# Expert products as four 32-column tiles with weight pieces of four experts, in a two-block transformer kernel

## The chip, the cores and the metric

The kernel runs on one core of a Trainium2 chip. The metric is the device time of one execution in microseconds.

## What is computed

Two transformer blocks on 256 tokens of width 1024 in float32. Block 1: attention with a forget gate beside a convolution, cross attention over 256 memory tokens, and a mixture of 32 experts. Block 2: a gated recurrence beside sparse attention, a wide MLP and a last gated product. The change touches the experts alone:

```python
gates = jnp.sum(jax.nn.one_hot(ids, N_EXPERTS) * w[..., None], axis=1).T   # each token: 2 of 32 experts
def expert_step(y, args):
    wg, wu, wd, ge = args                    # (1024, 512), (1024, 512), (512, 1024), (256,)
    out = (jax.nn.silu(t @ wg) * (t @ wu)) @ wd
    return y + ge[:, None] * out, None
y, _ = lax.scan(expert_step, jnp.zeros_like(t), (w_gate, w_up, w_down, gates))
```

Each expert has three matrices of 2.097 MB, 201 MB in all, each read once.

## The kernel before, in words

The program is raw: every engine has its own instruction list, and semaphores join them. Sums stand in eight PSUM banks (`ps`).

A token's place in its expert's list (`pos`) is worked out from the routing. Tokens of an expert are gathered by a product with a 0/1 matrix (`choose`), so that only they are multiplied: `CAP` = 64 places per expert. If the fullest expert (`busiest`) has more tokens, extra passes (`"more"`) run; with the given inputs its list is 26 long, so neither kernel runs them.

TensorE works on pairs of experts (`pair`, L759 to L805). For a pair n it does, in this order:
- `product` gate (L765): 8 row tiles of the 1024 inputs, for each a 128x64 block of gathered tokens (stationary) and 512 columns of the weights (moving). The two experts alternate and write the two halves of one bank (`ps[e * CAP:e * CAP + CAP, ...]`), that is, two column tiles of the array.
- `scatter` of the pair before (L778): four 128x512 matmuls that put expert outputs back to tokens, weighted by the gates; VectorE adds them to `x` (L1401). It has two banks, so the third and fourth wait for VectorE.
- `product` up, likewise; `gather` of the next pair (L749, 16 matmuls); four transposes of `hidden` (L792) and two of the weighted choice matrix (L798).
- `product` down: 4 row tiles, two banks of 512 columns.

ScalarE applies silu (L1889) and copies `hiddenT`, `spread` and the outputs out of PSUM (L1891 to L1896). A float32 matmul shows as two MATMUL and two LDWEIGHTS records in the trace.

**Weights.** SyncE loads one matrix of one expert per DMA (2.097 MB, `load_matrix`, L2111) into one of nine places of that size: three in the arena, six slots of the ring. Nine are loaded ahead, while block 1's last products still run. Each later one waits until the matrix that was in its place has been used; the semaphores for that count once per expert and product, and SyncE waits for both:

```python
sp.wait_ge(sem(f"{tag}_{used}_filled"), 2 * (PERIOD * group + u // 6 + 1))
```

The experts run in hardware loops of three pairs on each engine. After them SyncE waits for all products (`experts_done`), and then loads the weight units of block 2 (`load`, L2104, or by halves L2101): hq0 into slot 2, hq1 into slot 1, hf0 into slot 0, and the others as places come free. Block 2 starts with VectorE's norms (L1101 on) and TensorE's transposes (L516), then the product with hq0 (L555).

## Time and profile before

| | |
|---|---|
| median of 3 runs | 1447.36 us (1444.27 to 1447.55) |
| the profiled execution: its time | 1448.72 us |
| its span | 1446.9 us |
| TensorE busy | 1369.3 us (95%) |
| VectorE, ScalarE busy | 657.7, 414.7 us |
| granted TensorE clock, mean | 0.972 |
| HBM read | 330.4 MB, 229 GB/s over the span |
| chain that ended last | PE 85%, DVE 9%, ACT 2%, DMA 1%; L765 alone 23% |

In the profile PE is TensorE's matmul, PEld its weight load, DVE VectorE, ACT ScalarE, SP SyncE; SPq is SyncE's own queue. A granted clock of 1.00 is 2.4 GHz, 0.50 is 1.2 GHz.

### The profile page before, as it was taken

Reading aid. Unit: us, or ns where it says so; the run is one execution under the profiler, and the core shown is the slowest. Engines: PE = TensorE matmul, PEld = TensorE weight load, DVE = VectorE, ACT = ScalarE, POOL = GpSimd, SP = SyncE. Lnnn points to the kernel's source line nnn. Section 1 sums busy time; section 2 is a strip of 40 time slices with the busy share of each in tenths; the row PEclk is TensorE's granted clock in tenths of the full one; section 3 lists DMA queues with packets and bytes.
Section 4 is the critical chain, followed back from the end, with each engine's and each line's share of the span. In section 5 each row is a group of like instructions: output and inputs, shape, how many; then the busy total and the mean of one; then the engine's idle time right before and its main releaser. Section 6 shows DMA issues by size and latency. Waiting matters only on the chain.

```text
span 1446.9 us, 18297 instructions
## 1 busy us (share of the span) xinstructions
PE 1369.3 (95%) x7540; PEld 927.9 (64%) x7540; DVE 657.7 (45%) x1181; ACT 414.7 (29%) x626; POOL 14.1 (1%) x23
## 2 busy tenths in 40 slices
PE   6999999789999999999996999999999999999997
PEld 5977777454334443444333998887867746998873
DVE  3798532431122212121124358887656525655353
ACT  1343412101111111111111355634354302554322
POOL 2000000000000000000000000000000000000000
PEclk9997999889999999999998999999999999999999
DMA  8441464359999999999954153434433043455530
GB/s 332 176 159 75 168 248 166 143 222 401 420 427 425 425 419 426 426 423 425 421 232 176 54 193 119 158 132 146 186 135 117 1 167 117 175 182 194 206 145 29
DMA packets 26962, 332.45 MB, mean 230 GB/s; under 512 B 3184, under 2 KB 3472, under 8 KB 5008
## 3 DMA queue, kind: packets, MB, share of 16 engines
q1 hardware_dynamic: 25760, 328.49, 57.6%
q0 software_dynamic: 1136, 3.02, 0.6%
q8 instruction: 49, 0.80, 0.2%
q14 instruction: 17, 0.14, 0.0%
HBM read 330.44 MB, written 1.05 MB: 229 GB/s over the span
## 4 chain that ended last, share of the span: by engine, by line
PE 85%; DVE 9%; ACT 2%; issue 2%; DMA 1%; SPq 0%; DVEq 0%; ACTq 0%
PE ps L765 23%; PE ps L483 10%; PE ps L531 9%; PE ps L502 9%; PE ps L1016 6%; PE ps L555 6%; PE ps L749 5%; PE ps L778 4%; PE ps L446 2%; PE ps L845 2%; DVE arena L1193 1%; DVE parts L1149 1%; PE ps L607 1%; PE ps L578 1%; DMA ring<-in_units 1%
## 5 line engine op out<-in xcount | busy, mean ns | idle before, releaser
L765 PE MATMUL ps<-ring,arena 128*64 128x512 f32 x1008 | 260.8, 594 | 5.4 <-ACT arena L1891 5.4
L1149 DVE TENSOR_TENSOR parts<-ring,parts 128x2048 fp32r<-128x2048 f32 x76 | 173.5, 2290 | 156.7 <-ACT parts L1790 156.4
L1790 ACT CAST parts<-ring 128x2048 fp32r<-128x2048 f32 x76 | 144.4, 1904 | 178.1 <-PE ps L483 73.5
L502 PE MATMUL ps<-parts 128*128 128x512 f32 x768 | 181.6, 396 | 0.0
L765 PEld LDWEIGHTS ps<-ring,arena 128*64 128x64 f32 x1008 | 82.3, 137 | 144.4 <-issue 140.3
L483 PE MATMUL ps<-parts 128*128 128x256 f32 x1344 | 164.8, 285 | 3.1 <-DVE parts L1149 3.1
L483 PEld LDWEIGHTS ps<-parts 128*128 128x128 f32 x1344 | 163.4, 193 | 3.7 <-DVE parts L1149 2.1
L502 PEld LDWEIGHTS ps<-parts 128*128 128x128 f32 x768 | 145.7, 191 | 31.2 <-issue 1.1
L765 PE MATMUL ps<-arena 128*64 128x512 f32 x528 | 155.6, 594 | 3.3 <-ACT arena L1891 2.3
L1401 DVE TENSOR_TENSOR arena<-arena,ps 128x512 f32<-128x512 f32 x68 | 46.7, 687 | 236.8 <-PE ps L778 236.8
L531 PE MATMUL ps<-ring,arena 128*128 128x512 f32 x320 | 142.3, 602 | 4.4 <-issue 3.4
L531 PEld LDWEIGHTS ps<-ring,arena 128*128 128x128 f32 x320 | 60.9, 193 | 78.4 <-issue 77.2
L555 PE MATMUL ps<-arena,ring 128*128 128x128 f32 x768 | 93.9, 288 | 12.3 <-DMA ring<-in_units 6.9
L555 PEld LDWEIGHTS ps<-arena,ring 128*128 128x128 f32 x768 | 93.3, 204 | 14.2 <-issue 11.9
L765 PEld LDWEIGHTS ps<-arena 128*64 128x64 f32 x528 | 48.3, 137 | 79.6 <-issue 76.1
L1016 PE MATMUL ps<-parts 128*128 128x512 f32 x384 | 87.3, 389 | 0.0
L1016 PEld LDWEIGHTS ps<-parts 128*128 128x128 f32 x384 | 72.0, 188 | 14.9
L1891 ACT COPY arena<-ps 128x512 f32<-128x512 f32 x16 | 9.4, 585 | 230.6 <-PE ps L792 230.6
L749 PEld LDWEIGHTS ps<-arena 128*128 128x128 f32 x544 | 64.0, 197 | 15.0 <-issue 15.0
L749 PE MATMUL ps<-arena 128*128 128x128 f32 x544 | 67.2, 283 | 1.9 <-DVE arena L1380 1.9
L778 PE MATMUL ps<-arena 128*128 128x512 f32 x136 | 66.1, 618 | 1.3 <-ACT arena L1896 1.3
L1407 DVE TENSOR_TENSOR arena<-arena,ps 128x512 f32<-128x512 f32 x16 | 11.0, 687 | 101.9 <-PE ps L765 101.9
(313 smaller groups left out, 1231.3 us busy)
## 6 DMA issues: line engine op xcount, KB each, us to landing
ring<-in_units SPq DMA_DIRECT2D x43, 2048.0 KB, 7.7
ring<-in_w_down SPq DMA_DIRECT2D x22, 2048.0 KB, 12.9
ring<-in_w_up SPq DMA_DIRECT2D x21, 2048.0 KB, 12.0
ring<-in_w_gate SPq DMA_DIRECT2D x20, 2048.0 KB, 10.9
ring<-in_units SPq DMA_DIRECT2D x31, 1024.0 KB, 5.1
arena<-in_w_gate SPq DMA_DIRECT2D x12, 2048.0 KB, 11.5
arena<-in_w_up SPq DMA_DIRECT2D x11, 2048.0 KB, 11.4
arena<-in_w_down SPq DMA_DIRECT2D x10, 2048.0 KB, 12.1
```

What stands on the lines that cost most here:

```text
L446: mm = nc.tensor.matmul(bank, lhs[:, k, t * P:t * P + P], w[:, k, :], start=k == 0, stop=k == KT - 1)
L483: mm = nc.tensor.matmul(banks[f][:, half * T:half * T + T], w[:, k, at:at + P], v[:, 4 * h + k, :], start=h + half + k + n == 0, stop=h + ...
L502: mm = nc.tensor.matmul(banks[t], v[:, 4 * h + k, t * P:t * P + P], w[:, k, :], start=h + k + n == 0, stop=h == 1 and k == 3 and n == 2)
L531: mm = nc.tensor.matmul(bank, lhs[:, k, t * P:t * P + P], w[c][:, k, :], start=k == 0, stop=k == KT - 1)
L555: mm = nc.tensor.matmul(banks[u, c][:, to:to + P], w[u][:, k, at:at + P], rhs[:, k, t * P:t * P + P], start=k == 0, stop=k == KT - 1)
L749: mm = nc.tensor.matmul(ps[:, b, (k % 4) * P:(k % 4) * P + P], normed[:, t, k * P:k * P + P], choose[:, t, :], start=t == 0, stop=t == TT - 1)
L765: mm = nc.tensor.matmul(ps[e * CAP:e * CAP + CAP, bank, :], src[:, k, e * CAP:e * CAP + CAP], w[e][:, k, c * 512:c * 512 + 512], start=k = ...
L778: nc.tensor.matmul(ps[:, 5 + c, :], spread[:, t * P:t * P + P], expert_out[:, c * 512:c * 512 + 512], start=True, stop=True).then_inc(s("s ...
L1016: mm = nc.tensor.matmul(tiles[t], v[:, 4 * h + k, t * P:t * P + P], w[:, k, :], start=k4 + h + k + n == 0, stop=k4 == 3 and h == 1 and k = ...
L1149: step(V.tensor_tensor(rest_half(name, h), split_half(name, h), w_high[stage][h].bitcast(F32), ALU.subtract), f"{stage}_rest_ready", wait= ...
L1401: V.tensor_tensor(x[:, t, c * 512:c * 512 + 512], x[:, t, c * 512:c * 512 + 512], ps[:, 5 + c, :], ALU.add).then_inc(s("sum_drained"), 1)
L1790: step(S.copy(w_high[stage][h], split_half(name, h)), f"{stage}_high_ready", wait=False)
```

## The change

1. `CAP` goes from 64 to 32, and four experts (`SIDE` = 4, a quad; `QUADS` = 8) are worked on at once, as four 32-column tiles.
2. The weights are laid out anew on the host: a DMA brings a **piece** (2.097 MB as before), which holds two of the eight row tiles of gate or up for all four experts, or one of the four of down. 12 pieces to a quad, 96 in all, through the same nine places.
3. Each piece counts `piece_used` once per expert, and the next load into its place waits for that piece alone.
4. The scatter has four banks (`sum_banks`), and no wait inside. The choice matrices are built by one VectorE instruction instead of four.
5. The main expert stage is written out instead of looped (8 quads), on all engines.
6. SyncE issues the first three weight units of block 2 right behind the last piece, each after the last piece in its slot has been used, ahead of reading `busiest`.

```diff
-CAP = 64
+CAP = 32
+SIDE = P // CAP
-PAIRS = EXPERTS // 2
+QUADS = EXPERTS // SIDE
+PIECES = 12
...
+def quad_pieces(w, k):
+    n = w.shape[-1]
+    tiles = w.reshape(QUADS, SIDE, -1, k, P, n).transpose(0, 2, 4, 1, 3, 5)
+    return tiles.reshape(-1, P, SIDE * k * n)
...
-                    def product(group, r, first, tiles, name):
-                        src = hiddenT if first == 4 else picked
-                        for m in (6 * r + first, 6 * r + first + 1):
-                            landed, before = expert_landed(tag, m)
-                            pe.wait_ge(landed, before + 16 * (6 * PERIOD // N_PLACES * group + m // N_PLACES + 1))
-                        w = [expert_view(6 * r + first + e) for e in range(2)]
-                        n_k = src.shape[1]
-                        for c, bank in enumerate(tiles):
-                            for k in range(n_k):
-                                for e in range(2):
-                                    mm = nc.tensor.matmul(ps[e * CAP:e * CAP + CAP, bank, :], src[:, k, e * CAP:e * CAP + CAP],
-                                                          w[e][:, k, c * 512:c * 512 + 512], start=k == 0, stop=k == n_k - 1)
-                                    if c == len(tiles) - 1 and k == n_k - 1:
-                                        mm.then_inc(s(name), 1)
+                    def product(n, first, bank):
+                        for u in range(4):
+                            w = piece(n, first + u)
+                            for k in range(2):
+                                for e in range(SIDE):
+                                    mm = nc.tensor.matmul(ps[e * CAP:e * CAP + CAP, bank, :], picked[:, 2 * u + k, e * CAP:e * CAP + CAP],
+                                                          w[:, e, k, :], start=u + k == 0, stop=u == 3 and k == 1)
+                                    if k == 1:
+                                        mm.then_inc(s("piece_used"), 1)
...
+                    def down(n):
+                        pe.wait_ge(s("hiddenT_ready"), n + 1)
+                        for u in range(4):
+                            w = piece(n, 8 + u)
+                            for c in range(2):
+                                for e in range(SIDE):
+                                    mm = nc.tensor.matmul(ps[e * CAP:e * CAP + CAP, 3 + c, :], hiddenT[:, u, e * CAP:e * CAP + CAP],
+                                                          w[:, e, c, :], start=u == 0, stop=u == 3)
+                                    if c == 1:
+                                        mm.then_inc(s("piece_used"), 1)
...
-                                if t:
-                                    pe.wait_ge(s("sum_drained"), 4 * n + c + 1)
-                                nc.tensor.matmul(ps[:, 5 + c, :], spread[:, t * P:t * P + P],
+                                nc.tensor.matmul(ps[:, sum_banks[2 * t + c], :], spread[:, t * P:t * P + P],
...
+                    for n in range(QUADS):
                         pe.wait_ge(s("picked_drained"), 2 * n + 2)
+                        product(n, 0, 1)
+                        if n:
+                            scatter(n - 1)
+                        product(n, 4, 2)
+                        if n:
+                            pe.wait_ge(s("sum_drained"), 4 * n)
+                        if n + 1 < QUADS:
+                            gather(n + 1)
+                        turn_hidden(n)
+                        turn_spread(n)
+                        down(n)
+                    scatter(QUADS - 1)
...
-                load_pairs("moe", PAIRS)
+                n_places = places_of["moe"]
+                for m in range(n_places, PIECES * QUADS):
+                    sp.wait_ge(sem("moe_piece_used"), SIDE * (m - n_places + 1))
+                    load_piece("moe", m, m // PIECES, m % PIECES)
+                for n in range(n_early, n_early + 3):
+                    last_piece = max(m for m in range(PIECES * QUADS) if expert_places[m % n_places] == ("slot", units[n][2]))
+                    sp.wait_ge(sem("moe_piece_used"), SIDE * (last_piece + 1))
+                    load(n)
                 sp.wait_ge(sem("busiest_ready"), 1)
                 count = sp.value_load(busiest[0:1, 0:1], min_val=0, max_val=T)
-                experts_done("moe", PAIRS)
                 with sp.If(count > CAP):
```

TensorE, second group of experts, from its gate product over the scatter into the up product. Names in the rows: `moe_landed` and `weights_landed` are the semaphores of the places, and the loop of before shows each instruction once. Before:

```order
L759 REGISTER_ALU [waits moe_picked_drained]
L765 MATMUL ps<-ring,arena 64x512 [waits weights_landed1,weights_landed0]
L765 MATMUL ps<-ring,arena 64x512 x15
L778 MATMUL ps<-arena 128x512 [waits moe_out_ready,moe_spread_ready]
L778 MATMUL ps<-arena 128x512
L777 ISA
L778 MATMUL ps<-arena 128x512 [waits moe_sum_drained]
L777 REGISTER_ALU
L778 MATMUL ps<-arena 128x512 [waits moe_sum_drained]
L759 ISA [waits weights_landed2]
L765 MATMUL ps<-ring,arena 64x512 [waits moe_landed0]
```

Now, where `piece_used` is counted by the last matmuls of each piece:

```order
L777 MATMUL ps<-ring,arena 32x512 [waits weights_landed0]
L777 MATMUL ps<-ring,arena 32x512 x7
L814 MATMUL ps<-arena 128x512 [waits moe_out_ready,moe_spread_ready]
L814 MATMUL ps<-arena 128x512 x3
L777 MATMUL ps<-ring,arena 32x512 [waits weights_landed1]
L777 MATMUL ps<-ring,arena 32x512 x7
L777 MATMUL ps<-ring,arena 32x512 [waits weights_landed2]
L777 MATMUL ps<-ring,arena 32x512 x7
L777 MATMUL ps<-arena 32x512 [waits moe_landed0]
L777 MATMUL ps<-arena 32x512 x7
```

The product waits for one piece at a time instead of for two whole matrices, and the scatter's inner waits are gone.

SyncE, from the last of the nine loads ahead to the first that need a freed place. Before:

```order
L2111 DMA ring<-in_w_up 128x4096 [waits bank_filled3]
L2122 UNCONDITIONAL_BRANCH
L2122 ISA
L2111 ISA [waits moe_gate_filled]
L2111 DMA arena<-in_w_up 128x4096
L2111 ISA [waits moe_gate_filled]
L2111 DMA arena<-in_w_down 128x4096
L2111 DMA arena<-in_w_down 128x4096 [waits moe_up_filled]
```

Now:

```order
L2162 DMA ring<-in_w_up 128x4096 [waits bank_filled7]
L2162 DMA ring<-in_w_down 128x4096 [waits bank_filled3]
L2162 DMA arena<-in_w_down 128x4096 [waits moe_piece_used] x3
L2162 DMA ring<-in_w_gate 128x4096 [waits moe_piece_used] x4
L2162 DMA ring<-in_w_up 128x4096 [waits moe_piece_used] x2
L2162 DMA arena<-in_w_up 128x4096 [waits moe_piece_used] x2
```

The wait for a whole product of two experts has become a wait for one piece.

SyncE, from the last expert loads to the branch on `busiest`. Before (block 2's loads stand behind the branch):

```order
L2111 DMA ring<-in_w_up 128x4096 [waits moe_gate_filled]
L2111 DMA ring<-in_w_down 128x4096 [waits moe_gate_filled]
L2111 DMA ring<-in_w_down 128x4096 [waits moe_up_filled]
L2149 TENSOR_LOAD busiest [waits busiest_ready]
L2149 ISA x2
L2151 COMPARE_AND_BRANCH [waits moe_down_filled,moe_up_filled,moe_gate_filled]
```

Now:

```order
L2162 DMA arena<-in_w_down 128x4096 [waits moe_piece_used]
L2162 DMA ring<-in_w_down 128x4096 [waits moe_piece_used] x3
L2155 DMA ring<-in_units 128x4096 [waits moe_piece_used] x2
L2152 DMA ring<-in_units 128x2048 [waits moe_piece_used]
L2152 DMA ring<-in_units 128x2048
L2210 TENSOR_LOAD busiest [waits busiest_ready]
L2210 ISA x2
L2211 COMPARE_AND_BRANCH
```

Three units of block 2 (the third in two halves) stand ahead of the branch, and their only wait is for the pieces.

## Rows read from the trace of the kernel before

**Rows 1.** Page, 40 equal slices of the span (36.2 us each).
```profile
DMA  8441464359999999999954153434433043455530
GB/s 332 176 159 75 168 248 166 143 222 401 420 427 425 425 419 426 426 423 425 421 232 176 54 193 119 158 132 146 186 135 117 1 167 117 175 182 194 206 145 29
```

**Rows 2.** Windows: stretch, its us, busy us (instructions) per engine, granted clock, DMA share, GB/s.
```profile
275.00:280.00 5.00, 1.47 (x6) 0.90 (x5) 2.99 (x6) 0.20 (x1) 0.00 (x0) 0.77 0.70 223
280.00:285.00 5.00, 4.10 (x21) 3.73 (x19) 0.69 (x1) 3.02 (x8) 0.00 (x0) 0.50 1.03 439
295.00:300.00 5.00, 4.78 (x29) 4.58 (x28) 1.85 (x4) 1.28 (x1) 0.00 (x0) 0.69 0.00 0
305.00:310.00 5.00, 5.00 (x19) 1.84 (x16) 0.89 (x2) 0.60 (x1) 0.00 (x0) 1.00 0.25 52
330.00:335.00 5.00, 5.00 (x26) 1.78 (x24) 0.00 (x0) 2.36 (x3) 0.00 (x0) 1.00 0.71 229
335.00:740.00 405.00, 398.30 (x1942) 168.43 (x1938) 88.49 (x209) 51.03 (x81) 0.00 (x0) 1.00 1.01 424
740.00:745.00 5.00, 5.00 (x27) 1.59 (x24) 0.51 (x3) 0.00 (x0) 0.00 (x0) 1.00 0.63 265
745.00:775.00 30.00, 29.54 (x146) 12.38 (x144) 6.36 (x15) 3.81 (x6) 0.00 (x0) 1.00 0.00 1
```

**Rows 3.** Chain that ended last, one pair of experts: start us, us, what.
```profile
412.73 13.96 PE ps L765 x64
426.69 3.82 PE ps L778 x8
430.51 7.02 PE ps L765 x32
437.52 3.77 PE ps L749 x32
...
442.40 0.64 PE ps L765
```

**Rows 4.** Waits of TensorE (300 to 776 us) and SyncE: in total, times, longest.
```profile
PE ps L765 <- ACT arena L1891: 7.7, 16, 0.5
PE ps L765 <- DVE arena L1394: 1.0, 1, 1.0
...
SPq L2111 <- PE ps L765: 415.2, 44, 30.8
```

**Rows 5.** Timeline of SyncE and chain at the stage's start; loads of L2104 at 776.
```profile
300.76 1.04 PE ps L765 x3
...
308.04 0.35 SPq L2111 DMA_DIRECT2D arena<-in_w_up  x1
...
776.44 0.81 SPq L2104 DMA_DIRECT2D ring<-in_units  x2
...
DMA to landing us min/median/max: 8.0/10.6/13.1
```

**Rows 6.** Groups by line, 300 to 776 us: weight loads of the 64-column tiles.
```profile
L765 PEld LDWEIGHTS ps<-ring,arena 128*64 128x64 f32 x1008 | 82.3, 137 | 144.4 <-issue 140.3 <-ACT arena L1891 4.2
```

**Rows 7.** Page, DMA queue of the instruction fetches: packets, MB, share.
```profile
q8 instruction: 49, 0.80, 0.2%
```

**Rows 8.** Chain behind the last product of the experts.
```profile
773.97 2.20 PE ps L765 x10
...
776.82 0.46 ACT arena L1896
...
777.41 3.88 PE ps L778 x8
...
781.31 0.70 DVE arena L1401
...
783.22 1.22 DVE arena L1101
...
791.80 3.08 issue
```

More of the change, by code:

```diff
@@ L328, in two_blocks_kernel @@
                 before_experts = list(loads)
-                for m in range(6 * PAIRS):
-                    kind, at = expert_places[m % N_PLACES]
+                for m in range(PIECES * QUADS):
+                    kind, at = expert_places[m % places_of["moe"]]
                     if kind == "slot":
@@ L802, in experts @@
-                    with pe.Fori(0, n_pairs // PERIOD) as group:
-                        for r in range(PERIOD):
-                            pair(group, r)
-                    for r in range(n_pairs % PERIOD):
-                        pair(n_pairs // PERIOD, r)
-                    scatter(n_pairs)
-                    pe.wait_ge(s("sum_drained"), 4 * n_pairs + 4)
+                    return s, gather, product, turn_hidden, turn_spread, down, scatter
+                def experts():
+                    s, gather, product, turn_hidden, turn_spread, down, scatter = expert_steps("moe")
+                    gather(0)
+                    for n in range(QUADS):
+                        pe.wait_ge(s("picked_drained"), 2 * n + 2)
+                        product(n, 0, 1)
[10 more added lines that the diff above has]
+                    scatter(QUADS - 1)
+                    pe.wait_ge(s("sum_drained"), 4 * QUADS)
@@ new lines, in more_experts @@
+                def more_experts():
+                    s, gather, product, turn_hidden, turn_spread, down, scatter = expert_steps("more")
+                    with pe.Fori(0, MORE) as n:
+                        gather(n)
+                        pe.wait_ge(s("picked_drained"), 2 * n + 2)
+                        product(n, 0, 1)
+                        product(n, 4, 2)
+                        turn_hidden(n)
+                        turn_spread(n)
+                        down(n)
+                        scatter(n)
+                        pe.wait_ge(s("sum_drained"), 4 * n + 4)
@@ L816, in _ @@
                 with pe.If(count > CAP):
-                    experts("more", MORE)
+                    more_experts()
                 normed_half("mix2T", 0, 7)
@@ L1425, in experts @@
-                    drain_sums(n_pairs)
-                    dve.wait_ge(s("sum_drained"), 4 * n_pairs + 4)
-                experts("moe", 0, PAIRS)
+                    for n in range(QUADS):
+                        if n:
+                            drain_sums(n - 1)
+                        gate_hidden(n)
+                        if n + 1 < QUADS:
+                            drain_picked(n + 1)
+                            dve.wait_ge(s("spread_filled"), n + 1)
+                            build_gated(n + 1)
+                            dve.wait_ge(s("gated_choose_ready"), n + 2)
+                        if n + 2 < QUADS:
+                            build_choose(n + 2)
@@ L1429, in _, with more_experts @@
+                    drain_sums(QUADS - 1)
+                def more_experts():
+                    s, build_choose, build_gated, drain_picked, drain_sums, gate_hidden = expert_steps("more", QUADS)
+                    with dve.Fori(0, MORE) as n:
+                        build_choose(n)
+                        drain_picked(n)
+                        build_gated(n)
+                        gate_hidden(n)
+                        drain_sums(n)
+                experts()
                 count = dve.value_load(busiest[0:1, 0:1], min_val=0, max_val=T)
@@ L1430, in _ @@
                 with dve.If(count > CAP):
-                    experts("more", PAIRS, MORE)
+                    more_experts()
                 dve.wait_ge(sem("final_gain_landed"), 16)
@@ L1901, in _ @@
                 with act.If(count > CAP):
-                    experts("more", MORE)
+                    with act.Fori(0, MORE) as n:
+                        expert_quad("more", n)
                 for t in range(TT):
@@ new lines, in early_piece, with load_more_experts, load_next @@
+                def early_piece(m):
+                    load_piece("moe", m, m // PIECES, m % PIECES)
+                def load_more_experts():
+                    n_places = places_of["more"]
+                    def load_next(n, u):
+                        sp.wait_ge(sem("more_piece_used"), SIDE * (PIECES * n + u + 1))
+                        load_piece("more", u, n + (u + n_places) // PIECES, (u + n_places) % PIECES)
+                    sp.wait_ge(sem("moe_piece_used"), SIDE * PIECES * QUADS)
+                    for u in range(n_places):
+                        load_piece("more", u, 0, u)
+                    with sp.Fori(0, MORE - 1) as n:
+                        for u in range(PIECES):
+                            load_next(n, u)
+                    for u in range(PIECES - n_places):
+                        load_next(MORE - 1, u)
```

174 lines of the change are left out of this document (72 added, 102 removed).

## The prediction

> **What bounds the kernel now.** I read the page's slices first, then the windows of the expert stage, then the chain of waits inside it, then the waits of TensorE and SyncE. The slices show ten of the forty in which the DMA engines are full and move about 425 GB/s, with few others near that [rows 1]: this is the expert stage, a third of the span, and the change is in it. The windows put numbers on its two ends [rows 2]: from 335 to 740 us the DMA share is 1.01 at 424 GB/s, and TensorE is busy for 398.3 of 405 us. Both are full. Which of them sets the pace is told by the chain: it runs from one TensorE piece to the next, 13.96 + 3.82 + 7.02 + 3.77 us and some 1.1 us of transposes and handover, from 412.73 to 442.40: 29.67 us for a pair of experts [rows 3]. And TensorE's waits in the stage are 7.7 and 1.0 us in total, none for a DMA, while SyncE waits 415.2 us for TensorE's products to free a place [rows 4]. So TensorE is the bound, by a hair: six matrices of 2.097 MB in 29.67 us are 424 GB/s, just what the window shows.
>
> What TensorE costs is seen at the ends. SyncE's first load that needs a freed place goes out at 308.04, though the first product starts at 300.76, since a place comes free only after the whole gate product of two experts [rows 5]. The DMA engines rest between about 295 and 309 us (share 0.00, then 0.25), and again from 743 to 776 us (0.63, then 0.00), where all weights have landed and TensorE still works through a backlog [rows 2]. Block 2's loads go out at 776.44.
>
> **The sum.** It is made inside the profiled execution (span 1446.9, its own time 1448.7; the median of the runs shown is 1447.4, 1.3 lower, so the same difference is taken from the median).
>
> *TensorE's work per byte.* Two experts as 64-column tiles run side by side: 64 records of 128x512 take 13.96 us, 0.436 us for two. The change gives four tiles. If all four run side by side, a product of four experts takes the 7.0 us that two take now, and a group of four takes the 29.7 us of a pair, for twice the bytes. A weight piece (16 records) then takes 1.75 us. The trace has no 32-column tile, so the cost is bounded: below by 1.75 us; with never more than two at once 3.5 us; with no overlap 7.0 us; and if the 16 weight loads went singly, 16 x 137 ns = 2.2 us [rows 6]. A piece of 2.097 MB at 424 GB/s needs 4.95 us. In every case but the third the group (12 pieces plus about 8.8 us for gather, scatter, transposes and handover) stays under 12 x 4.95 = 59.4 us, and TensorE, the bound now, ends with slack: the DMA rate becomes the bound. I take 1.75, as the pair row shows full overlap of two.
> The Trainium skill (TensorE: Matmul & The Clock Gate, Part 3) gives 2.38x for three column tiles, short of 3x, which would make a piece 2.2 us instead of 1.75 and the sum 0.5 us longer; no run here shows it.
>
> *The start.* The choice matrix is now one VectorE instruction for four; worth a few tenths at most, taken as nothing. The first product starts at 300.8, its first piece is used at 302.5, and the first bound load goes out there instead of at 308.04: 5.5 us earlier. Pieces are used every 1.75 us against 4.95 us of transfer, so the dip at 330 to 335 us (229 GB/s) goes too.
>
> *The transfers.* 96 pieces less 9 preloaded are 87: 182.4 MB, at 424 GB/s 430.3 us [rows 2]. Two 2 MB loads into idle engines took at least 8.0 us each to land [rows 5], 3.1 more than 4.95. The last piece lands at 302.5 + 3.1 + 430.3 = 735.9. The same rule gives 308.0 + 3.1 + 430.3 + 2.3 (the dip) = 743.7 for the kernel before, where the DMA engines fell silent at 743.1. The loops written out bring more instruction fetches, about ten of 16 KB more (now 49 in the whole program, 0.80 MB [rows 7]): 0.2 MB, 0.4 us. Together 736.3.
>
> *The tail.* Behind the last product stand the two copies, the scatter, the last sum and VectorE's branch: in the trace 776.2 to 783.22, 7.0 us, of it 3.88 for the scatter [rows 8]. The last piece's product costs 1.75 us ahead of that, at full clock. But TensorE now works 1.75 of each 4.95 us. The granted clock was 0.77 in 275 to 280 us, where TensorE was busy 1.47 of 5, stayed at 0.50 in 280 to 285 with 4.10 of 5, and rose in 295 to 300 with 4.78 [rows 2]. So I take the lower level, 1.2 GHz, for the tail: the product 3.5 and the scatter 6.9 us (8 records at twice the 0.43 of full clock). At that level a group needs some 60 us of TensorE, about the 59.4 of its transfers; TensorE would then be busy without a break, and the clock would rise again, so the stage itself is not lengthened, and nine places cover the swings. Block 2's first instruction (L1101) starts at 736.3 + 3.5 + 1.2 + 6.9 + 0.7 + 1.2 = 749.8 instead of 783.22: 33.4 us saved, 38.6 at full clock.
> The Trainium skill (TensorE: Matmul & The Clock Gate, HAM oscillation) says that bursts of matmuls with a DMA wait between each find the clock low again every time; by it the low tail holds, and the trace's rows agree as far as they go.
>
> *Block 2's start.* Its first three weight units are queued behind piece 95 and land some 5, 10 and 15 us after it, by 751; TensorE wants the first about 8.6 us after L1101, at 758. Nothing waits for them, and nothing waited for them before either: their early issue is worth nothing by itself. But the chain has 3.08 us of "issue" at 791.80 that no engine releases, while the DMA engines are full with these units [rows 8]; I read it as an instruction fetch behind them, and with the queue empty by then I take half of it back: 1.5 us (bounds 0 and 3.1). The rest of block 2 is the same work, merely earlier.
>
> Sum: 33.4 + 1.5 = 35 us. 1448.7 - 35 = 1413.7 for a profiled run, 1447.4 - 35 = **1412.4** for the median.
>
> **The rivals.**
> *Warm tail (0.15).* The clock stays at 2.4 GHz: 5.2 us less, 1407. For it: a burst comes every 5 us; against it: the rows above.
> *The transfers run slower when never relieved (0.20).* Now leading DMA engines may catch their breath in the small slack; with the queue always eight deep the slowest engine sets the pace, and each of the ten added fetches delays one engine by about 1 us (0.2% of 16 engines' span over 49 packets). If all fall to the same engine this is 10 us; if the rate is 415 instead of 424 GB/s, 9 us. Time about 1423, at the worst 1430. For it: a DMA share of 1.01 leaves nothing in reserve; against it: 405 us at a flat 424.
> *Code starves TensorE (0.03).* If stalls like the 3.08 us one come with each of some 15 fetches of the stage and are not hidden, they cost 46 us against 35 won: about 1458, slower. Against it: a group has 29 us of slack for two such stalls, so they hide.
> *32-column tiles don't overlap (0.03), the slower end.* A piece costs 7.0 us, a group 12 x 7.0 + 8.8 = 92.8 us, the stage 742 instead of 475: about 1715. It decides from 4.2 us per piece (59.4 less 8.8, over 12). Overlap of two alone is not enough to get there: 50.8 us a group, and only 1.75 us more in the tail.
> *The change doesn't apply.* An expert with more than 32 tokens would call the extra passes, 56 groups of 59 us. From the given inputs the fullest expert has 26 tokens, so this is left out.
>
> **How the numbers follow.** The forecast case has 0.59 and its own range is 1406 to 1419 (rate 421 to 428 GB/s, the stall, the tiles at two). With the warm tail below and the slower transfers above, the range that should hold 8 in 10 is 1401 to 1427. A difference of 0.3% (4.3 us) is about what a measurement of this kernel can tell from none. Faster by more than that: 0.59 + 0.15 + 0.20 = 0.94; within: 0.01, a stretch between the cases in which stalls eat the gain; slower: the last two priced, 0.05.
>
> **What would show it.** Right: TensorE's largest waits in the stage are for DMA; SyncE's first load after a freed place near 302.5; DMA share 1.0 without a dip from there to 751, so that the idle stretch before block 2's loads is gone; TensorE busy near 50 to 70% with the clock under 1 in the stage; four L777 products inside 0.44 us at full clock; L1101 near 750. Wrong: landings further apart than 4.95 us, TensorE still without DMA waits, a piece over 4.2 us, or a gain that appears outside the stage.

## The result and the profile after

The changed kernel takes **1406.28 us** (median of 4 runs, 1399.48 to 1411.02) against 1447.4: a ratio of 0.9721, with a 95% interval of 0.9701 to 0.9741. The forecast was 1412.4, its range 1401 to 1427. The profiled execution is the fastest of the four: 1399.48 us, span 1397.2. Busy are TensorE 1180.7 us (1369.3 before), VectorE 593.5 (657.7), ScalarE 375.3 (414.7); the mean granted clock is 0.934 (0.972).

The page's slices (34.9 us each), to hold against [rows 1], with the granted clock; and the queue of the instruction fetches, against [rows 7]:

```profile
PEclk9997999979878989888788999999999999999999
DMA  9432283279999999999993443443441034445440
GB/s 342 183 127 115 98 324 127 78 304 428 427 428 428 427 428 428 427 428 427 428 427 148 146 170 121 154 143 127 181 181 61 32 142 159 187 187 190 182 151 30
...
q8 instruction: 58, 0.95, 0.3%
```

Twelve slices at 427 or 428 GB/s instead of eleven of 401 to 427; under them the clock wavers. The windows, against [rows 2] (stretch, its us, busy us of PE, PEld, DVE, ACT, POOL with their instructions, granted clock, DMA share, GB/s):

```profile
300.00:305.00 5.00, 5.00 (x48) 1.58 (x52) 0.70 (x2) 0.00 (x0) 0.00 (x0) 1.00 0.37 115
305.00:310.00 5.00, 5.00 (x52) 1.54 (x48) 0.00 (x0) 1.88 (x2) 0.00 (x0) 1.00 1.03 433
...
330.00:335.00 5.00, 1.92 (x16) 0.42 (x16) 0.00 (x0) 0.00 (x0) 0.00 (x0) 1.00 1.01 433
335.00:720.00 385.00, 247.78 (x1542) 74.79 (x1546) 36.85 (x58) 16.54 (x33) 0.00 (x0) 0.84 1.01 428
...
745.00:750.00 5.00, 1.47 (x7) 1.50 (x8) 4.43 (x9) 0.29 (x2) 0.00 (x0) 0.51 0.23 93
```

The full run of the DMA engines starts in 300 to 305 and has no dip at 330; it holds 428 GB/s. TensorE, busy for 398.3 of 405 us before, is busy for 247.8 of 385 us. In 745 to 750 the DMA engines fall silent with block 2's first units loaded. Before, they stood idle from 743 to 776 us.

The waits of TensorE in the stage (in total, times, longest), against [rows 4], and SyncE's longest one:

```profile
PE ps L777 <- DMA ring<-in_w_gate: 41.4, 19, 3.1
...
PE ps L803 <- DMA ring<-in_w_down: 30.3, 14, 3.0
...
PE ps L777 <- DMA arena<-in_w_up: 22.0, 8, 3.0
...
SPq L2162 <- PE ps L777: 262.7, 59, 24.8
```

TensorE waits for weights; before it never did. At the stage's start the chain (start us, us, what) and SyncE's timeline, against [rows 3] and [rows 5]:

```profile
299.99 13.94 PE ps L777 x128
313.93 3.77 PE ps L757 x32
...
302.06 3.76 SPq L2162 DMA_DIRECT2D arena<-in_w_down  x3
```

128 records of 32-column tiles take 13.94 us, what 64 records of 64-column tiles took before: **four tiles run side by side in full**. The first bound load goes out at 302.06 instead of 308.04. And the tail, against [rows 8]:

```profile
693.08 40.55 DMA ring<-in_w_down
...
733.67 2.05 PE ps L803 x16
...
736.96 3.69 PE ps L814 x8
...
742.57 1.22 DVE arena L1144
...
751.15 1.30 issue
752.45 2.69 PE ps L565 x11
```

The chain now runs through a DMA: the last piece, issued at 693.08, is there at 733.63. Its product, the copies, the scatter and the last sum follow, and block 2 starts at 742.57 instead of 783.22: 40.65 us earlier. Its first product starts at 752.45 instead of 794.88, 42.4 us earlier. The span is shorter by 49.7 us, so 7 us of this one trace come from behind, where nothing was changed. A gain outside the stage was one of the prediction's signs of being wrong; here it is a matter of this execution, as the repeats show.

### The profile page after: what moved, and what is told of

The parts are those of the page before. It is cut to its first block, busy times and chain, and to the rows that moved or that the text cites. A ratio compares the mean times of both kernels' runs of the same rounds, so it can differ in the third digit from the quotient of the medians.

```text
span 1397.2 us, 16587 instructions
## 1 busy us (share of the span) xinstructions
PE 1180.7 (85%) x7132; PEld 813.6 (58%) x7132; DVE 593.5 (42%) x992; ACT 375.3 (27%) x571; POOL 14.1 (1%) x23
## 4 chain that ended last, share of the span: by engine, by line
PE 59%; DMA 27%; DVE 10%; issue 2%; ACT 2%; SPq 0%; DVEq 0%; ACTq 0%
PE ps L493 10%; PE ps L541 9%; DMA ring<-in_w_up 9%; DMA ring<-in_w_gate 9%; PE ps L512 9%; PE ps L1059 6%; DMA ring<-in_w_down 6%; PE ps L565 6%; PE ps L777 3%; DMA arena<-in_w_up 3%; PE ps L456 2%; PE ps L888 2%; DVE arena L1236 1%; DVE parts L1192 1%; PE ps L617 1%
## 5 line engine op out<-in xcount | busy, mean ns | idle before, releaser
L777 PE MATMUL ps<-ring,arena 128*32 128x512 f32 x688 | 108.3, 763 | 65.7 <-DMA ring<-in_w_gate 41.4
L1437 DVE TENSOR_TENSOR arena<-arena,ps 128x512 f32<-128x512 f32 x32 | 22.0, 689 | 262.0 <-PE ps L814 261.9
L777 PEld LDWEIGHTS ps<-ring,arena 128*32 128x32 f32 x688 | 21.8, 125 | 148.8 <-issue 56.7
L565 PE MATMUL ps<-arena,ring 128*128 128x128 f32 x768 | 91.0, 282 | 11.2 <-DMA ring<-in_units 7.4
L565 PEld LDWEIGHTS ps<-arena,ring 128*128 128x128 f32 x768 | 90.2, 199 | 13.3 <-issue 11.0
L777 PE MATMUL ps<-arena 128*32 128x512 f32 x336 | 48.3, 704 | 37.8 <-DMA arena<-in_w_up 22.0
L803 PE MATMUL ps<-ring,arena 128*32 128x512 f32 x320 | 47.5, 721 | 32.6 <-DMA ring<-in_w_down 30.3
L1444 DVE TENSOR_TENSOR arena<-arena,ps 128x512 f32<-128x512 f32 x8 | 5.5, 688 | 120.2 <-PE ps L777 120.2
L777 PEld LDWEIGHTS ps<-arena 128*32 128x32 f32 x336 | 10.0, 117 | 75.1 <-DMA arena<-in_w_up 31.4
L1940 ACT COPY arena<-ps 128x512 f32<-128x512 f32 x8 | 4.7, 585 | 167.6 <-PE ps L786 167.6
L1236 DVE SCALAR_TENSOR_TENSOR arena<-arena,cols 128x256 f32<-128x256 f32 x120 | 48.6, 479 | 0.0
L803 PEld LDWEIGHTS ps<-ring,arena 128*32 128x32 f32 x320 | 9.3, 119 | 64.5 <-DMA ring<-in_w_down 46.0
```

What stands on the lines that cost most here:

```text
L565: mm = nc.tensor.matmul(banks[u, c][:, to:to + P], w[u][:, k, at:at + P], rhs[:, k, t * P:t * P + P], start=k == 0, stop=k == KT - 1)
L777: mm = nc.tensor.matmul(ps[e * CAP:e * CAP + CAP, bank, :], picked[:, 2 * u + k, e * CAP:e * CAP + CAP], w[:, e, k, :], start=u + k == 0, ...
L803: mm = nc.tensor.matmul(ps[e * CAP:e * CAP + CAP, 3 + c, :], hiddenT[:, u, e * CAP:e * CAP + CAP], w[:, e, c, :], start=u == 0, stop=u == 3)
L1236: ins = V.scalar_tensor_tensor(out=conv[:, cb, :], in0=z[:, cb, w:w + T], scalar=tap(w, cb), in1=conv[:, cb, :], op0=ALU.mult, op1=ALU.add)
```

## Experiments

Each edit is against the changed kernel unless another is named. There were twelve runs in three groups, each group on one chip beside the kernel before. The first group (a repeat of the changed kernel, the coarse wait, the late and the early units) and the third (a second repeat, the doubled and the tripled matmuls, the fillers at both ends) hold the changed kernel itself. The second (expert by expert, half loads, fillers at the start, fillers at the tail) does not, so its runs are compared with the changed kernel only by way of their ratios to the kernel before.

### The changed kernel, again

> The changed kernel again, unaltered, for a second trace of it and as the yardstick of the runs beside it. Theory (the transfers pace the expert stage): TensorE waits for DMA in the stage, the last piece lands near 733, and single times spread over some 10 us, because the granted clock falls and rises many times in the stage and its level in the tail, at 735 us, and in block 2 differs from run to run. The scatter then takes 3.7 us in one run and up to 6.9 in another. Rival (the first profile is typical, the spread is noise of the DMA rate): the tail is alike in both traces and the landing of the last piece moves by several us instead.

> The changed kernel once more, on the same chip as the three beside it, as their yardstick and for a third trace: median 1405 to 1410, single times spread over 10 us, with the level of the clock at 735 us and in block 2 going along with the time.

Medians 1408.57 (1402.78 to 1408.88, 5 runs, ratio to before 0.9709 to 0.9745) and 1407.73 us (1398.75 to 1409.68, 6 runs, 0.9697 to 0.9745). The second repeat's trace is of a run of 1408.11 us. Its chain at the tail:

```profile
732.01 3.01 PE ps L803 x16
...
736.26 5.36 PE ps L814 x8
...
743.54 1.22 DVE arena L1144
```

The last piece is there at 731.97, 1.7 us before that of the first trace (its loads began at 300.29, 1.8 us earlier); but product and scatter take 3.01 + 5.36 us against 2.05 + 3.69. In the first repeat the tail is as in the first trace, in the second it is slower. So the theory holds: the landing is steady, the clock is what changes. Block 2, from L1144 to the end of the span, took 1397.2 - 742.57 = 654.6 us in the first trace, 1400.5 - 741.24 = 659.3 in the first repeat and 1405.8 - 743.54 = 662.3 in the second. One window over the whole of block 2, first trace and then second repeat:

```profile
742.00:1397.00 655.00, 623.19 (x3730) 508.90 (x3730) 378.75 (x565) 265.74 (x380) 5.89 (x9) 0.98 0.37 138
```

```profile
742.00:1406.00 664.00, 631.02 (x3730) 514.91 (x3730) 379.04 (x566) 265.81 (x380) 5.91 (x9) 0.97 0.37 135
```

The same 3730 matmul records keep TensorE busy 7.8 us longer, at a mean clock of 0.97 instead of 0.98, while VectorE and ScalarE are busy for the same time in both. So what differs is how long the clock was low. The 662.3 us is the usual length: six of the variants below have 662.0 to 663.0. The kernel before had 1446.9 - 783.22 = 663.7. **So 7 to 8 us of the first trace's gain belong to that one run; the medians' 39 to 41 us are those of the stage.**

### When a place is given back

```diff
-                    sp.wait_ge(sem("moe_piece_used"), SIDE * (m - n_places + 1))
+                    sp.wait_ge(sem("moe_piece_used"), SIDE * (4 * ((m - n_places) // 4) + 4))
```

> A load waits again until the whole product (four pieces) that used its place is done, not the one piece; the rest is the changed kernel. Theory (the DMA rate bounds the stage and what counts is when its unbroken run begins): the first such load goes out 5.2 us later, near 307 instead of 302, the DMA engines stay full afterwards, and the whole is 5 us slower. Rival 1 (nine places absorb it): within 1 us. Rival 2 (the queue runs dry in each group, with only five to eight places in flight): slower by 2 us or more per group, 15 to 40 us in all.

1413.65 us (1413.18 to 1414.87), 5.1 slower than the repeat beside it (1408.57); ratio to before 0.9753 to 0.9785, against the repeat's 0.9709 to 0.9745, so clear of it. SyncE's first bound load in it, and its last piece's product:

```profile
304.93 1.28 SPq L2162 DMA_DIRECT2D arena<-in_w_down  x3
...
736.58 3.76 PE ps L803 x16
...
749.35 1.22 DVE arena L1144
```

4.05 us later than in the first repeat (300.88) and the last landing at 736.54 instead of 732.3, 4.2 us later. What the start lost came out at the end, no more and no less, so both rivals fall: nine places don't absorb it, and the queue doesn't run dry. (The 5.2 us expected are there too: the load goes out 7.21 us after the first product's start at 297.72, in the repeat 2.06 us after it; but that product happened to start 1.1 us earlier in this trace.)

### Block 2's units, late in the new kernel and early in the old

```diff
-                for n in range(n_early, n_early + 3):
-                    last_piece = max(m for m in range(PIECES * QUADS) if expert_places[m % n_places] == ("slot", units[n][2]))
-                    sp.wait_ge(sem("moe_piece_used"), SIDE * (last_piece + 1))
-                    load(n)
...
+                sp.wait_ge(sem("moe_piece_used"), SIDE * PIECES * QUADS)
+                for n in range(n_early, len(units)):
```

> The three weight units of block 2 are issued behind the branch on the fullest expert again, as in the kernel before, after all pieces are used; the rest is the changed kernel. Theory (early units are worth little, since TensorE wants the first of them 16 us after the last piece's product): 0 to 2.5 us slower than the changed kernel, all of it in the wait ahead of the first product of block 2 (1.3 us of issue there now, 3.1 before the change). Rival (the early units are a part of the gain, by filling the DMA engines' idle time): slower by 5 to 10 us, with TensorE waiting for ring<-in_units at the start of block 2.

1407.37 us (1405.47 to 1409.26), ratio to before 0.9706 to 0.9738: no difference from the repeat (1408.57). The units went out at 736.40 instead of 706.36, and TensorE's pause ahead of block 2's first product was 1.31 us, as with early units (1.30). **This part of the change is worth nothing that these runs can tell.**

The same part alone in the kernel before (the units behind `load_pairs`, each when the matrix in its slot is used):

```diff
                 load_pairs("moe", PAIRS)
+                for n, used in ((n_early, "down"), (n_early + 1, "down"), (n_early + 2, "up")):
+                    sp.wait_ge(sem(f"moe_{used}_filled"), 2 * (PAIRS - 1))
+                    load(n)
```

> The kernel before with nothing changed but that its three first units of block 2 are issued right behind the last expert matrix, as the change does. Theory: the gain of the change is not here; what goes is the 3.1 us of issue ahead of the first product of block 2, which I read as an instruction fetch that stands behind 6 MB of unit loads: 1.5 to 3 us faster than the kernel before. Rival (the units themselves are waited for): more than 5 us faster. Second rival (that stall has nothing to do with the DMA queue): no difference, and the 3.1 us still there.

1446.17 us against 1447.26, ratio 0.9996 (0.9987 to 1.0004): the second rival's "no difference" for the time, the theory for the pause. The DMA engines were idle by then (window 775 to 790), and the pause fell from 3.08 to 1.63 us:

```profile
775.00:790.00 15.00, 5.82 (x16) 2.80 (x16) 10.82 (x20) 2.92 (x8) 0.00 (x0) 0.80 0.01 3
...
789.39 1.63 issue
791.02 8.76 PE ps L555 x64
```

The late units above don't speak against a fetch behind the loads. In the kernel before the DMA engines were full for the first part of the pause, which began at 791.80; with late units in the changed kernel they had just run empty when it began, at 753.30 (first row before, second row late units):

```profile
792.00:793.00 1.00, 0.00 (x0) 0.00 (x0) 0.97 (x3) 0.00 (x0) 0.00 (x0) 0.50 0.99 410
...
753.00:754.00 1.00, 0.00 (x0) 0.00 (x0) 0.97 (x2) 0.29 (x2) 0.00 (x0) 0.50 0.14 57
```

So the pause was long in the one trace in which it met full DMA engines, and 1.30 to 1.63 us where it didn't. That it is an instruction fetch is not shown. With early units in the kernel before it is 1.45 us shorter; the interval allows the whole a gain of 1.9 us at most.

### How much TensorE may cost

Expert by expert inside a piece:

```diff
-                            for k in range(2):
-                                for e in range(SIDE):
+                            for e in range(SIDE):
+                                for k in range(2):
...
-                            for c in range(2):
-                                for e in range(SIDE):
+                            for e in range(SIDE):
+                                for c in range(2):
```

> Inside a piece the eight matmuls are issued expert by expert instead of row tile by row tile, so that two in a row go to the same 32-column tile. Same work, same loads. Theory (the gain rests on four tiles running side by side; TensorE becomes the bound from 4.2 us per piece): matmuls to one tile don't overlap, neighbours of two tiles do, a piece costs five steps of 0.86 = 4.3 us; a group costs about 60 us, no more than its transfers by 1 us, and the time grows by 0 to 15 us, with the clock at full level nearly throughout. Rival (a second matmul to the same tile stops all tiles): 7.0 us per piece, 93 us per group, 260 us slower. Rival 2 (order doesn't matter, the array takes what is ready): 1.75 us per piece, no change.

1407.76 us (1406.89 to 1410.43), ratio to before 0.9715 to 0.975, against 0.9697 to 0.9745 of the repeats: no change. My theory of this run fell and its second rival stands. The chain of its first two products:

```profile
300.07 14.01 PE ps L777 x128
```

128 records in 14.01 us. Two matmuls in a row to one tile don't hold up those of the next tile, as far as this time tells. As a test of the turning point the run is void.

Weights loaded by half (the matmuls of both row tiles, in the down product those of both banks, take the same half of the weights):

```diff
-                    src = by_piece[u // 4][:, bass.ds(4 * (quad % QUADS) + u % 4, 1), :]
-                    sp.dma_start(expert_flat(tag, m).unsqueeze(1), src)
+                    src = by_piece[u // 4][:, bass.ds(4 * (quad % QUADS) + u % 4, 1), 0:SLOT // 2]
+                    sp.dma_start(expert_flat(tag, m)[:, 0:SLOT // 2].unsqueeze(1), src)
...
-                                                          w[:, e, k, :], start=u + k == 0, stop=u == 3 and k == 1)
+                                                          w[:, e, :], start=u + k == 0, stop=u == 3 and k == 1)
```

> Each expert piece is loaded by half (1 MB), and the matmuls take their weights from that half, so the expert outputs are not those of the reference; the count of matmuls, waits and loads is the same. Theory (DMA bytes pace the stage): the stage shrinks from 433 to about 240 us, where TensorE (29.7 us per group at full clock) and the transfers (12 x 2.45 = 29.4 us) are level again, and the whole takes about 1215 us. Rival (a fixed cost per load or the instruction stream paces it): the stage shrinks by less than 100 us.

1202.45 us (one run, 13 less than expected), some 205 us less than the changed kernel; the last product ends at 530.3 instead of 735.7. The chain is TensorE alone again, one group of four from 407.77 to 437.23, 29.46 us where I had worked out 29.7:

```profile
407.77 7.07 PE ps L803 x64
414.85 6.87 PE ps L777 x64
421.71 3.63 PE ps L814 x8
425.34 7.01 PE ps L777 x64
432.35 3.77 PE ps L757 x32
...
437.23 2.77 PE ps L803 x23
```

So bytes pace the changed kernel's stage, and no fixed cost per load or instruction does.

Each expert matmul issued twice, and three times:

```diff
-                                for e in range(SIDE):
+                                for r, e in [(r, e) for r in range(3) for e in range(SIDE)]:
...
-                                                          w[:, e, k, :], start=u + k == 0, stop=u == 3 and k == 1)
-                                    if k == 1:
+                                                          w[:, e, k, :], start=u + k + r == 0, stop=u == 3 and k == 1 and r == 2)
+                                    if k == 1 and r == 2:
```

> Every matmul of the expert products is issued twice (the sums are doubled, so the expert outputs are not the reference's); loads and waits are as in the changed kernel. A piece then costs TensorE 3.5 us, a group 12 x 3.5 + 8.8 = 50.8 us against 59 us of transfers. Theory (the transfers pace the stage, TensorE has 29 us per group to spare): the last piece lands as before near 733, the clock stays at 2.4 GHz to the end of the stage, and the time is within 3 us of the changed kernel's 1406 to 1409. Rival (TensorE's work is still on the path in part): 20 us slower or more.

> Every matmul of the expert products is issued three times (sums tripled, outputs not the reference's). A piece costs 5.2 us, above the 4.2 us at which I put the turn: a group 12 x 5.2 + 8.8 = 71.6 us. Theory: TensorE is the bound again, its waits for DMA are gone, the stage takes 8 x 71.6 = 573 instead of 436 us, the whole about 1542 us. Rival (the turn lies higher, some of the repeats overlap as the matmuls of one tile did beside those of others): under 1450 us.

Twice: 1412.56 us (1404.52 to 1413.55, ratio 0.9722 to 0.9779), 4.8 more than the repeat beside it (1407.73), with intervals that overlap; the theory had said within 3 us of 1406 to 1409. The last piece landed at 736.94, not 733. Its first bound load went out at 302.48, 2.2 us later than the repeat's, and from there to the last landing it took 2.8 us more, which I put down, without a test, to places given back more slowly at the start. The window shows the clock:

```profile
335.00:720.00 385.00, 345.29 (x2936) 117.65 (x2932) 36.13 (x57) 16.86 (x33) 0.00 (x0) 1.00 1.01 427
```

TensorE is busy for 345 of 385 us, the clock is 1.00, and the transfers still go at 427 GB/s. The added 97 us of TensorE's busy time between 335 and 720 cost some 5 in all.

This run also tells which part of TensorE's saving is needed. With every matmul doubled, four experts' products cost 12 x 3.5 = 42 us by the prediction's terms, as much as the products of two pairs did before. What is still saved is that gather, scatter and transposes (some 8.8 us) come once for four experts instead of once for two. By these terms TensorE goes from 59.3 to 50.8 us for four experts, below the 59 us of their transfers. With that and the rest of the change in place 34 of the 39 us are gained, so the products' own halving adds little more than slack.

Three times: 1528.69 us (one run, 13 less than expected), with no waits of TensorE for DMA in the stage:

```profile
507.55 20.60 PE ps L777 x192
528.15 3.63 PE ps L814 x8
531.78 20.74 PE ps L777 x192
...
557.40 20.81 PE ps L803 x192
...
335.00:720.00 385.00, 382.26 (x3400) 133.25 (x3396) 31.07 (x50) 13.85 (x28) 0.00 (x0) 1.00 0.91 357
```

A product of four pieces takes 20.7 us, 5.2 per piece, a group 71 us; the DMA share falls to 0.91. Between 3.5 and 5.2 us per piece the bound goes over to TensorE. The 4.2 us of the prediction lie between them; closer than that it wasn't tried.

### The clock at the stage's two ends

Filler matmuls into a free bank, their result unused, in TensorE's waits:

```diff
+                def keep_busy(count):
+                    n = len(fills)
+                    if n >= BANKS:
+                        pe.wait_ge(sem(f"bank_drained{n % BANKS}"), n // BANKS)
+                    for _ in range(count):
+                        nc.tensor.matmul(ps[:, n % BANKS, 0:T], ident, const("ones"), start=True, stop=True)
...
+                keep_busy(7)
                 normed_half("ffnT", 1, 6)
...
+                keep_busy(8)
                 pe.wait_ge(sem("choice_ready"), 1)
```

(and 3 before the second turn of `ffnT`, 2 before the first gather.)

> The changed kernel with 20 filler matmuls (128x256, result unused) put into TensorE's waits between 275 and 293 us, ahead of the first expert product. Theory (what counts for the stage is when its first piece is used, and the clock is at 1.2 GHz there, which costs the routing product, the rank product and the first gather some 5 us): the clock stays at 2.4 GHz, the first piece is used 3 to 5 us earlier, and so is everything behind it. Rival (fillers delay the chain as much as the clock gives back, or don't hold the clock): no change or up to 3 us slower.

1404.56 us (1403.86 to 1408.31), ratio to before 0.9702 to 0.9737. Clock in the windows and SyncE's first bound load:

```profile
280.00:285.00 5.00, 5.00 (x32) 4.46 (x31) 2.78 (x15) 1.71 (x6) 0.53 (x1) 1.00 1.00 429
...
290.00:295.00 5.00, 5.00 (x34) 4.82 (x33) 0.69 (x1) 0.00 (x0) 0.00 (x0) 0.76 0.37 156
...
298.06 3.76 SPq L2175 DMA_DIRECT2D arena<-in_w_down  x3
```

The clock was 0.58 and 0.50 in these windows of the changed kernel's first trace and is 1.00 and 0.76, so it doesn't stay up all the way; the first bound load goes out at 298.06, 2.2 to 4 us before that of the three traces without fillers (300.29 to 302.06), and the last piece lands at 729.5 instead of 732 to 733.6. In the traces the theory holds, with 2.2 to 4 us where it forecast 3 to 5; the medians lie 2 to 4 us below those of the changed kernel in other groups, less than their intervals separate.

Fillers behind the last scatter instead:

```diff
+                keep_busy(12)
                 normed_half("mix2T", 0, 7)
+                keep_busy(3)
                 half_turned("mix2T", 0)
```

> The changed kernel with 15 filler matmuls (128x256, result unused) in TensorE's waits between the last scatter and the first product of block 2. Theory: the clock, which falls there at 745 and rises at 755 us, stays up; the transposes and the first product with hq0 run at 2.4 GHz and the whole is 2 to 4 us faster. Rival: the fillers stand in the way of the transposes, 1 to 3 us slower.

1405.11 us (1401.53 to 1413.08, ratio 0.9691 to 0.9725). Its traced run, the slowest, shows the rival at work:

```profile
743.00 4.76 issue
747.76 8.37 PE ps L434 x24
...
758.30 1.78 PE ps L573 x16
```

The fillers stand behind TensorE's read of `busiest` and its branch, and don't start until 4.76 us after the last sum. Then they run at the low clock, and block 2's first product starts at 758.30, 16.0 us after the last scatter's end. With late units, where product and scatter were as slow, it was 11.8 us. The median says neither: inconclusive.

Fillers ahead of the stage, and five before each piece of the last group's up and down products (the 6 in `fill(6)` is the bank, the count stays 5):

```diff
+                    def fill(bank, count=5):
+                        for _ in range(count):
+                            nc.tensor.matmul(ps[:, bank, 0:T], ident, const("ones"), start=True, stop=True)
...
                         for u in range(4):
+                            if tag == "moe" and n == QUADS - 1:
+                                fill(6)
                             w = piece(n, 8 + u)
```

> The changed kernel with the 20 filler matmuls ahead of the stage, and five more ahead of each piece of the last group's up and down products (40 in all, 128x256, results unused). Theory (the clock's level at both ends of the stage is worth time, in the stage it is not): the start as in the run with fillers there, 3 us, and the last product, scatter and copies at 2.4 GHz every time, 0 to 4 us by run: median 1400 to 1405, and a smaller spread of the single times. Rival (block 2's own falls of the clock outweigh it): the last scatter at full clock, yet the median within 1 us of the run with fillers at the start alone, 1404.6.

1403.61 us (1399.94 to 1404.59), ratio to before 0.9693 (0.9674 to 0.9712), against the repeat's 1407.73 and 0.9697 to 0.9745 beside it. The tail:

```profile
730.51 1.98 PE ps L824 x16
...
733.73 3.68 PE ps L835 x8
...
739.33 1.23 DVE arena L1166
```

The last product and scatter run at full clock (1.98 and 3.68 us), and block 2 starts at 739.33 instead of 741.2 to 744.7. Most of that is the start: the run with fillers there alone had block 2's start at 739.99, with its last product at 3.60 and its scatter at 3.69 us, so the fillers at the tail add 0.66 us in the traces. The median lies 4 us (0.3%) below that of the changed kernel beside it, with intervals that overlap, and 0.95 us below that of the fillers at the start alone, in another group. That meets the rival's "within 1 us" as well as the theory's 1400 to 1405: the runs don't decide between them. Faster than the kernel before it is by 2.9 to 3.3%; faster than the changed one only as far as the rows of the start and the tail show.

## Why the prediction was right, and where it was off

*The bound.* Right. TensorE set the pace with the DMA engines all but full behind it. With TensorE's products at half the time per byte the stage is bound by its bytes: the half loads give back 205 us, the doubled matmuls cost some 5. What runs after the first bound load is then a matter of transfers alone: from that load to the last landing it took 431.4 to 431.7 us in eight traces, the three of the changed kernel and those with the coarse wait, late units, expert by expert and fillers at either end (434.5 with doubled matmuls). Not tried apart are the four banks of the scatter, the single VectorE instruction and the loops written out; their share, if any, is within the same gain.

*TensorE's piece.* 1.75 us was right (13.94 us for eight pieces). In this trace a record of the four tiles costs 0.109 us, while a record of the scatter, which has the array to itself, takes 0.46 us at full clock: four tiles are about four times one, with float32 and 512 columns. By the Trainium skill's 2.38x for three column tiles (TensorE: Matmul & The Clock Gate, Part 3) my estimate had been 2.2 us; the measurement does not bear it out here. It would have changed the sum by 0.5 us.

*The start.* Forecast 302.5, measured 302.06, 300.88 and 300.29 in three traces. The experiment with the coarse wait confirms that every microsecond here comes out at the end.

*The transfers.* The rate made the term 4 us too long: I took 424 GB/s from the window of before, 430.3 us; with TensorE out of the way the engines give 428, 426.2 us. So 424 was TensorE's pace and not the engines' limit: my own first part said so (six matrices in 29.67 us are 424 GB/s), and the sum then used it as the engines' rate. The rest fits: 302.06 + 3.1 + 426.2 = 731.4, and 2.3 us remain, of which the fetches (58 instead of 49 packets, put at 0.4 us) may be a part; the rest is open. The stretch as a whole was forecast at 433.8 us and took 431.6. The last piece landed at 733.6 and not 736.3. The rival that a queue never relieved runs slower was wrong: it runs at 428.

*The tail.* The low clock was taken for the whole of it: 3.5 + 6.9 us. The traces have 2.05 + 3.69, 2.05 + 3.69 and 3.01 + 5.36 in the three runs of the changed kernel, and 3.76 + 5.16 with late units: the clock is low in some of the tail in some of the runs, since in the stage it goes up and down (0.84 on average). Over the eight traces named above the last product took 2.05 us twice, 3.01 once and 3.60 to 3.81 five times, the scatter 3.69 three times and 5.09 to 5.85 five times. So the product was mostly at the low clock, as forecast, and the scatter never for its whole length (6.9 us). The two quick tails belong to the fastest of the changed kernel's runs in their groups (1399.48 and 1402.78 us), so the first trace flatters the warm case. That is the forecast's and the rival's case mixed; at L1144 the first trace is 7.2 us ahead of my 749.8, of it 2.7 from the landing and 4.7 from product and scatter. The Trainium skill's oscillation between low and full clock under DMA waits (TensorE: Matmul & The Clock Gate, HAM oscillation) is seen here as a row: 0.84 over 385 us. That each burst finds the clock low is not. Two pieces of the first trace, one after the other, each behind the same wait:

```profile
709.19 1.92 PE L777 MATMUL ps<-arena 128*32 128x512 f32 x16 [2.97 <-DMA arena<-in_w_up]
714.07 3.44 PE L777 MATMUL ps<-arena 128*32 128x512 f32 x16 [2.96 <-DMA arena<-in_w_up]
```

*Block 2's start.* The pause of 3.08 us became 1.30, 1.8 us against the 1.5 taken; half was a choice between bounds, and its reason, a fetch behind the unit loads, fits the runs but is not shown. That the early units themselves are worth nothing was right, tried from both sides, within what the intervals can tell.

*The sum.* In the traces the gain up to block 2's first instruction is 40.65 us (42.0 and 39.7 in the repeats), against 33.4. The median moved by 41.1 us (38.7 and 38.9 in the repeats' batches) against 35. In the first trace the two reasons are those above, the rate and the tail's clock. In the second repeat, the more usual one, block 2 starts 6.3 us ahead of the forecast: 2.2 by the start, 4.1 by the rate and 1.9 by the tail, less some 2.0 that the transfers took beyond the terms named.

## What to carry to other kernels

When two resources are both full, take the one off that the chain of waits names, and expect to gain only up to the other: here TensorE's time per byte was cut, further than was needed, and the gain is what the DMA engines had idled at the stage's two ends, plus the 1% by which their own rate is above TensorE's pace. Take the rate of the next bound from a stretch where nothing holds it back, not from the mean of a stretch that another engine paced. And in a stage bound by its bytes what counts is when the unbroken run of transfers begins: give a buffer back by the piece, and bring the first use forward.

## What was not expected of the hardware

- Two matmuls in a row to one 32-column tile don't measurably delay those to the other tiles behind them: 128 records take 13.94 us in turn and 14.01 us by twos.
- The rate was 428 GB/s with a median of 41 us from issue to landing, and the same 428 with the coarse wait, where it was 31 to 34 us: a longer queue of 2 MB loads neither slowed the transfers nor sped them up. The 424 GB/s of the kernel before came with 11.5 to 12.9 us, but there TensorE set the pace; what the engines give at that depth when nothing else holds them is not shown.
- In a stage where TensorE is busy for two thirds of the time the granted clock goes up and down between its levels, and what it is at the end of the stage differs from run to run. The single times of the kernel before spread by 3 to 7 us in a batch, those of the changed kernel by 6 to 12. The same block 2 took 654.6 to 662.3 us in three traces, by how long the clock was low in it.
- With fillers right behind the read of `busiest` and the branch, TensorE's first matmul came 4.76 us after the last sum (743.00), VectorE's first instruction behind its own branch only 1.2 us after it. The cause is not shown. In the changed kernel TensorE waits there for VectorE's norms, and the trace doesn't say how much of this is hidden.
